# First norm of a two-block decoder step: its root moved from the input to the product banks

## What is computed

```
def rmsnorm(x, g):
    y = x32 * lax.rsqrt(jnp.mean(x32 * x32, axis=-1, keepdims=True) + EPS)
    return (y * g.astype(jnp.float32)).astype(x.dtype)
def rglru_layer(x, norm_g, w_in, conv_w, conv_b, wr, br, wi, bi, lam, w_out):
    h = rmsnorm(x, norm_g)
    u = h @ w_in
    xb, gate = u[..., :LRU_WIDTH], u[..., LRU_WIDTH:]
    xb = causal_depthwise_conv(xb, conv_w, conv_b)
    ...
    log_a = -LRU_C * r * jax.nn.softplus(-lam.astype(jnp.float32))
    ...
    y = hs.astype(x.dtype) * jax.nn.silu(gate)
    return x + y @ w_out
```

## Time and profile before

| what | value |
|---|---|
| median of 3 runs | 786.76 us (786.7 to 786.82) |
| the profiled execution | 786.78 us, of which the span is 784.9 us |
| PE busy | 776.7 us (99%) |
| DVE, ACT, POOL busy | 585.6 (75%), 488.0 (62%), 106.9 us (14%) |
| granted TensorE clock | full speed in all slices |

### The profile page before, as it was taken

One profiled execution on the slowest core, in us unless ns is written; L12 is line 12 of the kernel. 1 busy time (PEld: TensorE's weight loads), 2 busy tenths in 40 slices (PEclk: granted clock), 3 DMA queues, 4 the chain that ended last, 5 costly groups with the idle time before them and its releaser, 6 DMA issues.

```text
span 784.9 us, 14573 instructions
## 1 busy us (share of the span) xinstructions
PE 776.7 (99%) x5321; PEld 711.4 (91%) x5321; DVE 585.6 (75%) x892; ACT 488.0 (62%) x761; POOL 106.9 (14%) x195
## 2 busy tenths in 40 slices
PE   9999999999999999999999999999999999999997
PEld 8999999998998888888888899999999888888885
DVE  5989997978868887776459664796588887787443
ACT  7799946788675655554346565764756665555334
POOL 9697100157100000000000031000000000000000
PEclk9999999999999999999999999999999999999999
DMA  8663565633646766666665544445555676665651
GB/s 264 188 181 118 171 212 161 211 112 110 188 126 181 226 191 187 187 195 202 190 189 163 185 147 151 127 144 161 182 165 157 195 213 189 195 184 184 195 178 54
DMA packets 101557, 136.57 MB, mean 174 GB/s; under 512 B 5320, under 2 KB 86912, under 8 KB 101504
## 3 DMA queue, kind: packets, MB, share of 16 engines
q1 hardware_dynamic: 99232, 133.23, 55.4%
q0 software_dynamic: 2112, 2.54, 1.3%
q10 hardware_dynamic: 160, 0.07, 0.1%
HBM read 134.78 MB, written 1.05 MB: 173 GB/s over the span
## 4 chain that ended last, share of the span: by engine, by line
PE 91%; DVE 4%; ACT 3%; issue 1%; DMA 0%; ACTq 0%
PE bank L595 30%; PE bank L658 20%; PE bank L660 11%; PE bank L603 8%; PE bank L704 8%; PE bank L751 5%; PE bank L752 3%; DVE w_lo L1729 2%; DVE arena L1942 1%; PE bank L945 1%; PE bank L927 1%; ACT arena L1216 1%; PE bank L952 1%; ACT w_hi L1216 1%; ACT acts L1216 1%
## 5 line engine op out<-in xcount | busy, mean ns | idle before, releaser
L1729 DVE TENSOR_TENSOR w_lo<-stage,w_hi 128x1024 fp32r<-128x1024 f32 x249 | 305.3, 1231 | 124.5 <-ACT w_hi L1216 123.9
L1216 ACT ACTIVATE w_hi<-stage 128x1024 fp32r<-128x1024 f32 (+1 forms) x251 | 262.5, 1052 | 117.5 <-PE bank L595 41.7
L595 PE MATMUL bank<-acts,w_hi 128*128 128x256 f32 x1520 | 277.6, 285 | 0.9 <-DVE w_lo L1729 0.4
L658 PE MATMUL bank<-acts,w_hi 128*128 128x512 f32 x704 | 244.8, 392 | 0.0
L595 PEld LDWEIGHTS bank<-acts,w_hi 128*128 128x128 f32 x1520 | 236.5, 192 | 3.6 <-issue 1.7
L595 PE MATMUL bank<-acts,w_lo 128*128 128x256 f32 x760 | 214.9, 283 | 0.0
L660 PE MATMUL bank<-acts,w_lo 128*128 128x256 f32 x704 | 197.2, 280 | 0.0
L658 PEld LDWEIGHTS bank<-acts,w_hi 128*128 128x128 f32 x704 | 131.7, 187 | 29.2
L595 PEld LDWEIGHTS bank<-acts,w_lo 128*128 128x128 f32 x760 | 145.6, 192 | 0.0
L660 PEld LDWEIGHTS bank<-acts,w_lo 128*128 128x128 f32 x704 | 133.1, 189 | 0.0
L1216 ACT ACTIVATE arena<-bank 128x512 f32<-128x512 f32 (+1 forms) x79 | 43.6, 561 | 63.6 <-PE bank L660 45.9
(11 more groups left out here) (221 smaller groups left out, 810.2 us busy)
## 6 DMA issues: line engine op xcount, KB each, us to landing
stage<-ffn_w_gate SPq DMA_DIRECT2D x44, 512.0 KB, 4.2
stage<-ffn_w_up SPq DMA_DIRECT2D x44, 512.0 KB, 4.4
stage<-ffn_w_down SPq DMA_DIRECT2D x44, 512.0 KB, 3.8
stage<-w_in SPq DMA_DIRECT2D x40, 512.0 KB, 3.6
stage<-a_w_in SPq DMA_DIRECT2D x24, 512.0 KB, 4.6
stage<-b_w_in SPq DMA_DIRECT2D x16, 512.0 KB, 3.7
stage<-a_w_out SPq DMA_DIRECT2D x12, 512.0 KB, 3.7
stage<-b_w_out SPq DMA_DIRECT2D x8, 512.0 KB, 3.5
```

Of the source, the lines that this page charges most:

```text
L595: mm = pe.matmul(dst, w[:, slot, c:c + P], a[:, k, :] if isinstance(k, int) else a[:, bass.ds(k, 1), :], start=start and n == 0, stop=stop ...
L658: pe.matmul(two[p][:, m, :], w_hi[:, half % RING, c:c + P], wide(acts[:, k, :, :]), start=k == 0, stop=False, skip_group_check=True)
L1216: return nc.scalar.activation(out_, in_, func, **kw)
L1729: dve.tensor_tensor(w_lo[:, n % RING, 0:w], src, w_hi[:, n % RING, 0:w].bitcast(F32), ALU.subtract)\
```

## The change

x is loaded as two halves of its width (all 256 tokens each), with the two weight halves of x chunk 0 between and behind them on SP. PE turns each half of x once, unscaled, into banks 0 to 3, 6 and 7 (`turned_x`), ahead of all products; `a_hi` and `a_lo` are made from those banks, and the residual copies are taken from the same banks later. The root is worked out during x chunks 0 and 1, spread over the partitions by two PE products (`first_roots`) and copied to `spread`. Each x chunk's bank is then multiplied by `spread` on DVE into SBUF (`x_scale`, into `XU`), and the convolution's ACT and DVE operations read that; banks 4 and 5 come free after `x_scale` and not after the convolution. All six G chunks are copied out with the same multiplication (`gate_out`); before, DVE copied three and ACT read the other three from their banks. The softplus series is done on GpSimd in 17 steps behind the first gate weights. In the DVE and ACT loops the weight half of a step that ends a chunk is converted ahead of the convolution (before: behind it). Fourteen small loads go from GpSimd's queue to SP's.

```
+            def first_turns(first):
+                for k in range(first, first + 4):
+                    for tb in range(TB):
+                        mm = pe.transpose(turned_x(k)[:, tb * P:(tb + 1) * P], x_tok[:, tb, k * P:(k + 1) * P], ident)
+                    mm.then_inc(xt_done, 1)
...
             for c in range(6):
-                if c == 1:
-                    pe.wait_ge(par_ready, 1)
                 if c >= 2:
-                    pe.wait_ge(conv_x, 2 * (c - 1))
-                col_chunk(C_X + c, 4 + c % 2, normed=0)
...
+                    pe.wait_ge(x_scaled, c - 1)
+                if c:
+                    col_chunk(C_X + c, 4 + c % 2)
+                else:
+                    first_chunk()
+                    pe.wait_ge(par_ready, 2)
                 if c == 3:
                     pe.wait_ge(x_ready, 4)
                 if c in (3, 4):
                     gates(c - 3)
...
-                if n not in x_end and n:
+                if n:
                     hi(n + 4)
                 act.wait_ge(ring_free, n + 1)
                 if n in x_end:
                     c = x_end[n]
-                    if c == 0:
-                        act.wait_ge(par_ready, 2)
+                    act.wait_ge(x_scaled, c + 1)
                     for m in range(2):
                         t = 2 * c + m
-                        f(tiles(XB + t), bank[4 + c % 2][:, m * T:(m + 1) * T], ACT.Identity,
+                        f(tiles(XB + t), x_unit(c)[:, m * T:(m + 1) * T], ACT.Identity,
...
                     if c == 0:
-                        input_out(2)
-                        input_out(3)
-                        hi(4)
-                    hi(n + 4)
+                        input_out(7)
+                    elif c < 3:
+                        input_out(2 * c - 2)
...
+            def x_scale(c):
+                dve.wait_ge(ring_free, half_of(C_X + c) + 2)
+                rooted(XU + 2 * (c % 2), 4 + c % 2).then_inc(x_scaled, 1)
...
                 if n in x_end:
                     c = x_end[n]
+                    x_scale(c)
+                    if c == 0:
+                        dve.wait_ge(lam_e, 2)
+                        dve.tensor_scalar(lam[:, 2, :], lam[:, 1, :], 2.0, 1.0, ALU.add, ALU.mult).then_inc(lam_den, 1)
+                    lo(n + 4)
```

More of the change, by code:

```diff
@@ L512, in _ @@
[L512 to L518, removed]
@@ L521, in decay_square @@
+            pool.wait_ge(set_done, 5)
+            pieces(0, 0, 12)
+            pieces_again(0)
+            decay_scale()
+            pieces(1, 0, 4)
+            stack(0)
+            stack(1)
+            pieces(1, 4, 12)
+            pieces_again(1)
             def decay_square(g):
@@ L616, in turn_ahead, with first_roots @@
+            def first_roots():
+                pe.wait_ge(rstd_ready, 1)
+                pe.wait_ge(x_ready, 1)
                 for tb in range(TB):
-                    mm = pe.transpose(bank[5 + k % 3][:, tb * P:(tb + 1) * P], x_rst[:, tb, k * P:(k + 1) * P], ident)
-                mm.then_inc(xt_done, 1)
+                    mm = pe.matmul(bank[6][:, tb * P:(tb + 1) * P], n_rstd[:, tb:tb + 1].to_broadcast([P, P]),
+                                   ident, start=True, stop=True)
+                mm.then_inc(first_rb, 1)
@@ L620, in col_half @@
             def col_half(chunk, h, b, first_tile=0, normed=None, ready=None, token=False):
                 half = half_of(chunk) + h
[L625 to L628, removed]
+                pe.wait_ge(w_done, half + 1 if ready is None else ready)
                 for kk in range(4):
                     k = 4 * h + kk
[L631 to L635, removed]
+                    if chunk == C_X + 1 and k == 5:
+                        first_roots()
@@ L789, in _ @@
             pe.transpose(bank[7][:, 0:KD], rows_n[:, :], con[0:KD, IDENT:IDENT + KD]).then_inc(par_t, 1)
[L790 to L796, removed]
+            pe.wait_ge(x_in[0], 16)
+            first_turns(0)
             warm(WARM[1])
-            turn_ahead(0)
-            turn_ahead(1)
+            pe.wait_ge(x_in[1], 16)
+            pe.wait_ge(par_ready, 1)
+            first_turns(4)
             def gates(g):
@@ L1857, in _, with first_weights @@
-            normalised_lo(2)
-            normalised_lo(3)
-            lo(1)
-            for k in range(4, KD):
-                normalised_lo(k)
+            def first_weights(h, part):
+                dve.wait_ge((w_first_hi, hi_done)[part], h + 1)
+                at = slice(part * 2 * T, (part + 1) * 2 * T)
+                dve.tensor_tensor(w_lo[:, h, at], stage[:, 0, h, at], w_hi[:, h, at].bitcast(F32), ALU.subtract)\
+                    .then_inc((w_first, w_done)[part], 1)
+            dve.wait_ge(x_in[0], 16)
@@ new lines, in _ @@
+            dve.wait_ge(ms_part_d, 2)
+            dve.tensor_tensor(n_ms[:, :], fin_ms[:, 0:2], fin_ms[:, 2:4], ALU.add).then_inc(ms_ready, 2)
+            dve.wait_ge(par_ready, 2)
+            root_inv(0)
+            lo(4)
+            dve.wait_ge(first_rb, 1)
+            dve.tensor_copy(spread[:, :], bank[6][:, 0:T]).then_inc(first_sb, 1)
+            dve.wait_ge(first_sb, 1)
+            def x_scale(c):
+                dve.wait_ge(ring_free, half_of(C_X + c) + 2)
+                rooted(XU + 2 * (c % 2), 4 + c % 2).then_inc(x_scaled, 1)
```

335 lines of the change are left out of this document (175 added, 160 removed).

## The result

The changed kernel takes 797.5 us (median of 4 runs, 796.52 to 797.94) against 786.73 for the kernel before (4 runs, 786.46 to 786.82): a ratio of 1.0136, with an interval from 1.0124 to 1.0148. It is slower, as forecast, but by 10.8 us and not by 5.2, and it lies above the range. The profiled execution has a span of 795.6 us against 784.9. One run of the experiments (e2_fill, 1081.52 us at a mean granted clock of 0.655) was in a slow state throughout and is left out of its comparison.

What follows compares the result with a forecast made beforehand. PE was taken as the bound, movable only by its stream's start and its feeders DVE and ACT. A 3.2 us head start turned into half 20 being 5.2 late: 786.78 + 5.2 = 792.0 us, range 786.5 to 795.0.

Steps and rivals of the forecast that it cites:

- the start: First products: begin at about 8.8 us instead of 9.95, half 2 at 14.7 instead of 17.90, 3.2 us gained.
- the root: Root on ACT at 16.4 to 16.7 us, first x_scale at about 19.25, taps of chunk 0 at 21.6 against 19.48.
- The head start: PE's early start: 3.2 us at half 2, 2.1 left at half 6, first gate group at 35.4 against 35.25.
- The round: DVE and ACT work per x chunk: 6.75 us, 7.05 by the upper bound, where PE needs 5.76 for two halves.
- They end at 3.9: Six taps in the round of one x chunk: finished 3.9 us after x_scale starts, having started at 1.8.
- I take 2.1: Time for six taps with SBUF input: 2.1 us, from some 0.41 each.
- the upper bound that I had: Highest time allowed for the six taps: 2.42 us, taken from the bank.
- Worse: Rival: taps at 0.47 in four rounds, slow series, longer lo beside GpSimd's CASTs; 794 to 797 us, chance 0.13.
- The 5.2 us from start to start: Round of one x chunk before the change: DVE's tap, lo, xb_lo, lo without waiting, 5.2 us.
- I give it no case of its own: Granted clock falling in PE's new waits (up to 2.7 us at half 20): would add loss, but was given no price.
- I let the loss stand: Behind half 20: the 5.2 us lateness stays to the end; it could be 0 to 2 more.
- I take nothing off: Series leaving DVE's rounds: no gain counted, because the new round is 6.75 us without those small operations.

Runs made afterwards that it cites:

- e2_fill: Changed kernel with the next half's weight conversions ahead of xb_hi on ACT and xb_lo on DVE, filling DVE's waits: 793.72 us (1.0086).
- e4: Changed kernel with x_scale of chunks 2 to 5 written back into its own bank, from which bias and taps read: 794.93 us (1.0101).
- e1: Changed kernel without GpSimd's 32 restacking CASTs (zeros copied once instead, so gate groups lack the cross terms): 796.98 us (1.0129).
- e6: Changed kernel with 8 throwaway PE products before half 10 and 13 before half 20: 796.31 us (1.0122).
- e12: Changed kernel with x_scale left out, so the six x chunks stay unscaled and taps and bias read the banks: 790.18 us (1.0047).
- e13: Changed kernel with x_scale left out and the old order put back in the rounds: 787.51 us (1.0011).
- e5: Kernel before with only its rounds in the new order, and half 4 converted ahead of the first convolution too: 791.91 us (1.0066).
- e9: Changed kernel with its rounds in the old order, weight conversion behind bias and taps: 798.15 us (1.0144).
- e11: Changed kernel with only the series of the decay put back on VectorE in rounds 3 to 10: 798.52 us (1.0154).
- e10: Changed kernel with early root, filled order, in-place x_scale, earlier residual copies and gate loads, but the series back on DVE: 792.42 us (1.007).
- e8: Changed kernel with early root, filled order, in-place x_scale from chunk 2, earlier residual copies, six gate loads ahead of the series: 790.95 us (1.0059).
- e3: Changed kernel with 12 throwaway PE products before half 10 and 20 before half 20: 797.38 us (1.0136).
- e7: Changed kernel with squares and root made as each half of x lands, first_roots following at once: 797.05 us (1.0136).

## Why the prediction was right in direction and too small

**What bounds the kernel, the start and the root: right.** The first product came at 8.93 (8.8), `x_scale(0)` at 19.56 (19.25), its taps at 21.54 (21.6), half 6 at 27.45 (27.3). The head start was 2 us at half 6 and gone at the first gate group, as worked out.

**The round: right in its parts, wrong in one term.** The failed step is "They end at 3.9", from "I take 2.1". The term of the taps measured 2.4 alone, which is the upper bound that I had and did not take, and 3.0 to 3.3 beside GpSimd, which was in no bound: the bound came from the bank, the operand kind that e4 shows not to suffer. Half 20 was 3.7 us later than forecast. With 2.4 for 2.1 the rounds of chunks 0 to 3 give 1.3 of it, and GpSimd beside chunks 2 and 3 another 1.4 (0.8 and 0.6 above 2.45). In chunk 5 the taps run beside ACT's decay, and only what outlasts it counts, some 0.5 with the wait of 0.40 us ahead of `xb_hi`. The last 0.5 lies in small terms, such as a `lo` of up to 1.34 us beside the CASTs instead of 1.22, and PE starting 0.15 us behind the end of `lo` and not 0.05. The rival "Worse" (794 to 797, chance 0.13) came nearest, but 797.5 lies above it too. It had the taps at 0.47 and a longer `lo` beside the CASTs, but gave the taps no longer time beside them. The Trainium skill (GPSIMD Engine Reference, Key points) says that GpSimd contends with instructions of two SBUF inputs. By e1 and e4 it does, at 0.6 to 0.8 us for six taps. The Trainium skill (VectorE: DVE Perf Modes, the section on the TRN2 errata) has a fixed cost of 58 cycles from SBUF and 120 from PSUM, and adds that the row with them under-predicts single operations. By it the taps would have been faster from SBUF; measured they are equal, 2.38 to 2.46 us against 2.36 to 2.43, and the measurement decides.

The 5.2 us from start to start for the round before is the shortest case: the earlier trace rows has its taps 7.1 us apart in the first round, and the next are 5.4 and 6.2 apart. The sum compared starts of halves and not rounds, so this did not enter it.

**The clock: the step "I give it no case of its own" failed.** It was named as what could add to the loss, but priced at nothing. The wait before half 20 was forecast at up to 2.7 us and was 3.10, and behind it the granted clock was 0.50 for some 3 us: 1.26 us by its products, 1.2 by e6.

**The loss behind half 20: "I let the loss stand" was right but for the clock**, with 0.5 us more to the end of the span, inside the 0 to 2 that I had named.

The sum of the forecast, 5.2, so becomes 5.2 + 3.7 + 1.3 + 0.5 = 10.7, the growth of the span. **The cause** was the one named: the round. e12 prices the scaling at 7.3 us, in which the contention of the taps and the fallen clock at half 20 are contained, since its taps read banks and its clock stays at 1.00 there. e13 prices scaling with order at 10.0; the order alone is 5.2 in the kernel before (e5, with its later first convolution), 2.7 once the scaling is out (e12 to e13) and nothing with the scaling in (e9), so these prices must not be added up. **"I take nothing off" for the series was right**: the rounds of the forecast have no series in them, and putting it back made the medians 1.0 and 1.5 us longer (e11, e10), which is not clear of the noise. Its 17 steps took 8.2 us on GpSimd where I took 5. What stays open is how the cost divides between scaling and order, which depends on what else is in the round, and the split of the last 0.8 us of e13 between the first convolution and the gate loads.

## What to carry to other kernels

Deferring a scale from the input to the products moves it from the start, where it cost 3 us once, into every round of the loop; there it costs its own duration and also the cover that the operation behind it loses, so work out the round from start to start with each operation's cover named, before counting what the start wins. When two engines share a round, price SBUF operations of two inputs with the third engine beside them, and take the bound from rows of the same operand kind. If the forecast holds a new wait of 2 to 3 us of TensorE, give the fallen clock behind it a term of its own.

## What the runs showed of the hardware

- Six dependent taps of 255 columns with both large inputs in SBUF take 2.38 to 2.46 us alone or beside GpSimd's 12-column steps, and 3.04 to 3.29 beside its CASTs or its multiply of 768 columns in the changed kernel (2.67 in e9 to 3.67 in e2). With one input in a bank they take 2.36 to 2.43 in either case.
- An operation on one side can last until one on the other side has ended. The first tap of chunk 5, 1.32 us, ends 0.28 us after GpSimd's multiply, and the square in e1, 3.22 us, 0.55 us after the CAST of zeros. GpSimd's operations on 12 columns mostly take 0.20 to 0.32 us, but up to 1.10 in the changed kernel and 2.04 in e8; the one of 1.10 ends at 26.86 us and DVE's `lo` beside it at 26.80 (25.57 and 1.23), as the one in e8 ends with an `xb_lo`:

```profile
25.76 1.10 POOL L552 TENSOR_SCALAR lam<-lam 128x12 f32<-128x12 f32 x1
```

- After waits of 2.38 and 1.89 us with 3.9 us of work between, and around the end of one of 3.10 us, TensorE was granted 0.50 (1.2 GHz) for some 3 us, products 0.21 us apart. The same came with single waits of 2.32 (e4), 2.38 (e6), 2.66 (e12) and 2.54 us (e10), and with one of 4.54 (e2) for twice as long. No such stretch followed the waits of 1.54 us in the changed kernel, 1.95 in e5, 2.29 and 2.20 in e8, and 2.38 in e1. Products on constants in the waits of e3 kept it at 1.00. The length of a wait alone does not decide it: in the profiled execution of e7, waits of 1.95 and 1.89 us and one of 3.11 left the clock at 1.00, in the same places. What does was not found.
